# Three of seven block products with a 512-column operand of both residual parts, and two sums on VectorE in place of accumulation

## The chip, the cores and the metric

One core of a Trainium2 chip runs the whole program. The metric is the device time of one execution in microseconds; the median of three timed runs is taken. TensorE multiplies and adds up in PSUM (8 banks, each of 512 fp32 columns on 128 partitions), VectorE (DVE) and ScalarE (ACT) read PSUM and SBUF, GpSimd (POOL) SBUF only. The engines run their own queues in order and meet through semaphores.

## What is computed

The reference is a two-layer encoder over 512 tokens of width 1024. Each layer has two feed-forward halves (so four in all) around a mixer, and a gated embedding at its end. The change touches the feed-forward halves alone:

```python
def swiglu(h, w_gate, w_up, w_down):
    return (jax.nn.silu(h @ w_gate) * (h @ w_up)) @ w_down

h = h + 0.5 * swiglu(rms_norm(h, norms[i, 0]), ffn_w_gate[i, 0], ffn_w_up[i, 0], ffn_w_down[i, 0])
```

`w_gate` and `w_up` are 1024 x 2816, so gate and up together are 22 tiles of 128 rows each.

## The kernel before

**Precision.** Each fp32 operand is split into a high part (type fp32r, made by ACT with a copy) and a low part (the rest, made by DVE with a subtraction). A product of weight w and activation x is three matmuls: w_hi x_hi, w_hi x_lo, w_lo x_hi.

**Stages.** A feed-forward half f has an "up" stage of 22 tiles and a "down" stage. Six up tiles are plain (`in_chunk`, 512 columns). The other sixteen are *fast tiles*: gate and up weights of one tile form a 2 x 2 block matrix, which is multiplied with the 2 x 2 blocks of the normalised residual in seven block products in place of eight (Strassen's scheme). One block product is 4 blocks of 128 rows by 3 matmuls of 256 columns (`product`, L2284 to L2292). The sixteen tiles run as a static opening tile, one static tile, a hardware loop of two tiles per turn and, on DVE and ACT, a static end (`last_tile`).

**TensorE's order within a fast tile** (L2307 to L2328) is B11, T1, T2, B21, T3, B22, T4. B11, T2, T3, T4 add up in the tile's first bank; T1 and B22 in its right bank; B21 stands alone in its left bank. Two sets of three banks take turns. Since the first bank's partial sums are also needed, ACT copies them out between the products (`copy_part` 0, 1, 2, 3 after B11, T1, T2, T3), and TensorE waits for `copy_part` 0 before T2, for 2 before T3 and for 3 before T4.

**VectorE's order in a tile b** (`fast_tile`, L580) is: three weight sums for tile b+1 (`weight_sums`: w_sum 0:2 with 1024 elements, then two of 512 that each wait for the one before), low part of the sums T2 and T4 (`sums_lo` 0, which waits for ACT's high part), `gate_left`, low part of B11 and B21 (`own_lo` 0), `up_right`, low part of T1 and T3 (`sums_lo` 1), low part of B22 (`own_lo` 1), `up_left`, `product` (silu(gate) times up, written to `act_f`).

**ScalarE's order** (L1769) is: `copy_part` 0, 1, 2, high part of T2 and T4 (`sums_hi` 0, after the third weight sum and after T2), high part of B11 and B21 (`own_hi` 0), `copy_part` 3, `sums_hi` 1, `silu_left`, `own_hi` 1, `silu_right` (reads the first bank after T4). In `last_tile` (L1782) two copies of a finished tile's product, `act_high` 0 and 1, stand ahead of `copy_part` 0.

Each of these is one instruction on an in-order queue, so an instruction that waits holds all that stands behind it.

Of the kernel before, what the change touches and what calls it, by code (L numbers as in the profile page):

```python
# [24 lines left out]
P = 128  # L25
# [117 lines left out]
def encoder(nc, A, out):  # L143

    with ExitStack() as ctx:
        def sb(name, shape, dt=F32):
            where = nc.sbuf_base
            return ctx.enter_context(nc.sbuf_tensor(name, shape, dt)), where
# [3 lines left out]


        h, _ = sb("h", [P, KD, T])
        x_hi, at_x = sb("x_hi", [P, KD, T], F32R)
        x_lo, at_x_lo = sb("x_lo", [P, KD, T], F32R)
        act_hi, at_hi = sb("act_hi", [P, NF * T], F32R)
        act_lo, at_lo = sb("act_lo", [P, NF * T], F32R)
        raw, _ = sb("raw", [P, SLOTS, BLOCKS, P])
# [20 lines left out]
        def over(name, shape, where, dt=F32):  # L180

            return nc.alloc_sbuf_tensor_at(name, shape, dt, offset=where)
# [92 lines left out]
        act_f = over("act_f", [P, NF * T], at_lo)  # L275
        xn = over("xn", [P, KD, T], at_lo + 6 * tile_bytes)
        x_sum = over("x_sum", [P, 4, KH, HALF], at_lo + 14 * tile_bytes)
        xs_hi = over("xs_hi", [P, 4, KH, HALF], at_hi + 6 * tile_bytes, F32R)
        xs_lo = over("xs_lo", [P, 4, KH, HALF], at_hi + 14 * tile_bytes, F32R)
        corner_hi = over("corner_hi", [P, KH, HALF], at_hi + 2 * tile_bytes, F32R)  # L280
        corner_lo = over("corner_lo", [P, KH, HALF], at_hi + 4 * tile_bytes, F32R)
        part_sum = over("part_sum", [P, 4, T], at_x)
# [43 lines left out]
            "gate_scaled", "silu_done", "up_scaled", "prod_done", "act_hi_ready", "act_ready")}  # L326
        fast = {n: sem(f"fast_{n}") for n in (
            "x_gained", "x_normed", "x_sums", "x_hi", "x_ready", "w_sums", "t_hi",
            "t_ready", "product", "copied")}
        tab = sem("tab")  # L330
        tab_act = sem("tab_act")
        tab_pe = sem("tab_pe")
# [54 lines left out]
        def counted(each, f, i, b, n):  # L387

            return i * (2 * each) + (each * (b - PLAINS[f] + FAST_BEFORE[f]) + n)
# [11 lines left out]
        def banks_of(b):  # L401

            return ((5, 6, 7), (0, 1, 2))[b % 2]
# [41 lines left out]
        def act_low(dve, f, t):  # L445

            dve.wait_ge(ffn_sems["act_hi_ready"], t + 1 + NF * f)
            span = slice(t * T, (t + 1) * T)
            dve.tensor_tensor(act_lo[:, span], act_f[:, span], act_hi[:, span].bitcast(F32), SUB)\
               .then_inc(ffn_sems["act_ready"], 1)  # L450
# [5 lines left out]
        def ffn_up_dve(dve, f, n, first):  # L456
# [60 lines left out]
            def gate_left(i, b):  # L517
                dve.wait_ge(fast["product"], counted(5, f, i, b, 4))
                dve.wait_ge(fast["copied"], counted(4, f, i, b, 1))
                dve.tensor_tensor(t1[:, b % 2, 0:HALF], ps[:, banks_of(b)[1], 0:HALF],  # L520
                                  part_sum[:, 0, HALF:], ADD).then_inc(s["gate_scaled"], 1)

            def up_right(i, b):
                dve.wait_ge(fast["copied"], counted(4, f, i, b, 4))
# [2 lines left out]

            def up_left(i, b):
                dve.wait_ge(chunk_used, i * 4 + (first + 2 * b + 1))
                dve.tensor_tensor(t2[:, b % 2, 0:HALF], ps[:, banks_of(b)[2], 0:HALF],  # L530
                                  part_sum[:, 2, HALF:], ADD).then_inc(s["up_scaled"], 1)

            def product(i, b):
                dve.wait_ge(s["up_scaled"], i * 2 + (b + 1) + NF * f)
# [33 lines left out]
            def opening_tile():  # L568

                weight_sums(pair, 1)  # L570
                gate_left(pair, 0)
                own_lo(pair, 1, 0)
                sums_lo(pair, 1, 1)
                up_right(pair, 0)
                sums_lo(pair, 1, 0)
                own_lo(pair, 1, 1)
                up_left(pair, 0)
                product(pair, 0)

            def fast_tile(i, b):  # L580

                weight_sums(i, b + 1)
                sums_lo(i, b + 1, 0)
                gate_left(i, b)
                own_lo(i, b + 1, 0)
                up_right(i, b)
                sums_lo(i, b + 1, 1)
                own_lo(i, b + 1, 1)
                up_left(i, b)
                product(i, b)  # L590

            def last_tile(i, b):

                act_low(dve, f, 0)
                act_low(dve, f, 1)
                gate_left(i, b)
                split_lo(dve, first, FFN_UP)
                up_right(i, b)
                split_lo(dve, first, FFN_UP + 1)
                up_left(i, b)  # L600
                product(i, b)

            def passage_of_six():
# [1081 lines left out]
        def ffn_up_act(act, f, n, first, split=True):  # L1685
# [50 lines left out]
            def silu_right(i, b):  # L1736
                act.wait_ge(chunk_used, i * 4 + (first + 2 * b + 2))
                act.wait_ge(s["prod_done"], i * 2 + (b - 1) + NF * f)
                act.activation(t1[:, b % 2, HALF:], ps[:, banks_of(b)[0], 0:HALF], ACT.Silu)\
                   .then_inc(s["silu_done"], 1)  # L1740

            def residual_hi(o):
# [522 lines left out]
        def ffn_up_pe(pe, f, n, first):  # L2265
            s = ffn_sems

            if n == 4:
                for j in range(2):
                    in_chunk(pe, first, j, j, n=n, rows=range(KD - 1))  # L2270
                squares(pe, n)
                for j in range(2):
                    in_chunk(pe, first, j, j, n=n, rows=range(KD - 1, KD))
            plain = PLAINS[f]
            for j in range(2 if n == 4 else 0, 2 * plain):
                t, half = divmod(j, 2)
                before = [e for e in range(t) if PLAIN_BANKS[e] == PLAIN_BANKS[t]]
                if before:
                    pe.wait_ge(s[("gate_scaled", "up_scaled")[half]], before[-1] + 1 + NF * f)
                in_chunk(pe, first, j, PLAIN_BANKS[t][half], n=n if j == 0 else None)  # L2280
                if j == (0 if n in SQUARED else 1):
                    squares(pe, n)

            def product(bank, at, hi, lo, start, stop, done):  # L2284
                for k in range(KH):
                    cols = slice(k * P, (k + 1) * P)
                    for part, (w, x) in enumerate(((wf_hi, hi), (wf_hi, lo), (wf_lo, hi))):
                        last = pe.matmul(ps[:, bank, 0:HALF], w[:, at, cols], x[:, k],  # L2288
                                         start=(start and k == 0 and part == 0),
                                         stop=(stop and k == KH - 1 and part == 2),  # L2290
                                         skip_group_check=True)
                last.then_inc(done, 1)  # L2292

            def fast_tile(i, b):

                first_bank, left_bank, right_bank = banks_of(b)
                at = halves_of(first, b)

                def mixed(o):
                    return xs_hi[:, o], xs_lo[:, o]  # L2300

                def unmixed(o):
                    if o == 4:
                        return corner_hi, corner_lo
                    return quarter(x_hi, o), quarter(x_lo, o)

                pe.wait_ge(split_ready, i * 4 + (first + 2 * b + 1))  # L2307
                pe.wait_ge(fast["x_ready"], 7 * f + 5)
                pe.wait_ge(s["silu_done"], i * 2 + (b - 1) + NF * f)
                product(first_bank, at["B11"], *unmixed(4), True, False, fast["product"])  # L2310
                turned = isinstance(i, int) and 2 * i + b < plain + 2
                pe.wait_ge(fast["t_ready"], counted(2, f, i, b, 1 if turned else 2))
                pe.wait_ge(s["up_scaled"], i * 2 + (b - 1) + NF * f)
                product(right_bank, at["T1"], *mixed(0), True, False, fast["product"])
                if turned:
                    pe.wait_ge(fast["t_ready"], counted(2, f, i, b, 2))
                pe.wait_ge(fast["copied"], counted(4, f, i, b, 1))
                product(first_bank, at["T2"], *mixed(1), False, False, fast["product"])
                pe.wait_ge(fast["x_ready"], 7 * f + 6)
                pe.wait_ge(s["gate_scaled"], i * 2 + (b - 1) + NF * f)  # L2320
                product(left_bank, at["B21"], *unmixed(5), True, True, fast["product"])
                pe.wait_ge(fast["copied"], counted(4, f, i, b, 3))
                product(first_bank, at["T3"], *mixed(2), False, False, fast["product"])
                pe.wait_ge(split_ready, i * 4 + (first + 2 * b + 2))
                product(right_bank, at["B22"], *mixed(3), False, True, chunk_used)
                pe.wait_ge(fast["x_ready"], 7 * f + 7)
                pe.wait_ge(fast["copied"], counted(4, f, i, b, 4))
                product(first_bank, at["T4"], *unmixed(6), False, True, chunk_used)  # L2328

            fast_tile(plain // 2, 0)  # L2330
            fast_tile(plain // 2, 1)
            with pe.Fori(plain // 2 + 1, NF // 2, 1) as i:
                fast_tile(i, 0)
                fast_tile(i, 1)
# [601 lines left out]
```

## Time and profile before

| | |
|---|---|
| median of 3 runs (lowest to highest) | 1893.31 us (1892.08 to 1893.46) |
| profiled execution, its own time | 1893.9 us |
| its span, from the first to the last instruction | 1892.1 us |
| mean granted TensorE clock | 0.997 of 2.4 GHz |
| TensorE matmul busy | 1862.7 us (98%) |
| VectorE busy | 1342.0 us (71%) |
| ScalarE busy | 879.8 us (46%) |
| GpSimd busy | 261.3 us (14%) |
| share of the chain that ended last, by engine | PE 91%, DVE 6%, ACT 2%, POOL 1% |

Times are microseconds unless marked ns. PE is TensorE, PEld its weight loads, which overlap the matmuls. L12 is line 12 of the kernel before. The "chain" is followed back from the last instruction: at each step to what released it, or to the instruction before it on its engine. A matmul's duration in a row is its latency in the pipeline; how fast matmuls follow one another is read from the distance of their starts. The same holds for VectorE and ScalarE, where the next instruction can start a little before the one before has ended.

### The profile page before, as it was taken

The numbers are of one execution on the slowest core, as the hardware profiler recorded it, in microseconds if no ns is written. First come the engines' busy times: TensorE is split into PE (matmuls) and PEld (weight loads), VectorE is DVE, ScalarE is ACT, GpSimd is POOL, SyncE is SP. The second block draws the span as 40 slices with busy tenths as digits, with TensorE's granted clock in tenths as the row PEclk, the third lists the DMA queues.
The fourth block names the chain that finished last, engine by engine and source line by source line (L and its number), as shares of the span: only waits on it lengthen the run. The fifth ranks groups of instructions, "written<-read, shape, count | busy, mean of one in ns | idle before, by whom it ended". The sixth has DMA issues, their size and how long they took to land.

```text
span 1892.1 us, 30948 instructions
## 1 busy us (share of the span) xinstructions
PE 1862.7 (98%) x11274; PEld 1611.9 (85%) x11274; DVE 1342.0 (71%) x1957; ACT 879.8 (46%) x1475; POOL 261.3 (14%) x204
## 2 busy tenths in 40 slices
PE   8999999999999999999999999999989999999998
PEld 6899988777799998887899998877658899998886
DVE  8788788774878874357888864279984878874355
ACT  7455542245545554224455553234563645554222
POOL 0000001312100000224000001173243100000225
PEclk9999999999999999999999999999999999999999
DMA  5333333333223333323333343332101323333321
GB/s 179 90 111 96 105 104 104 95 99 91 78 87 104 111 102 120 105 74 100 101 91 99 111 122 95 94 109 68 56 1 45 94 88 108 111 102 121 102 76 56
DMA packets 56754, 179.90 MB, mean 95 GB/s; under 512 B 12144, under 2 KB 12144, under 8 KB 56656
## 3 DMA queue, kind: packets, MB, share of 16 engines
q1 hardware_dynamic: 54656, 173.69, 30.6%
q0 software_dynamic: 928, 3.02, 0.5%
q10 hardware_dynamic: 1088, 2.10, 0.3%
q8 instruction: 52, 0.85, 0.2%
q14 instruction: 30, 0.25, 0.0%
HBM read 175.04 MB, written 3.15 MB: 94 GB/s over the span
## 4 chain that ended last, share of the span: by engine, by line
PE 91%; DVE 6%; ACT 2%; POOL 1%; issue 0%; DMA 0%; DVEq 0%; SPq 0%; POOLq 0%; ACTq 0%
PE ps L2288 34%; PE ps L2250 26%; PE ps L2232 22%; PE ps L2736 2%; PE ps L2399 1%; PE ps L2635 1%; DVE sm L1265 1%; DVE work L1241 1%; POOL sumsq L1541 1%; PE ps L2685 1%; DVE stat L1239 1%; DVE x_lo L436 1%; PE ps L2654 0%; ACT prob L1970 0%; PE ps L2450 0%
## 5 line engine op out<-in xcount | busy, mean ns | idle before, releaser
L384 DVE TENSOR_TENSOR w_lo<-raw,w_hi 128x1024 fp32r<-128x1024 f32 x182 | 241.4, 1335 | 219.7 <-ACT w_hi L376 218.7
L376 ACT ACTIVATE w_hi<-raw 128x1024 fp32r<-128x1024 f32 x194 | 202.2, 1054 | 306.1 <-PE ps L2250 248.8
L2232 PE MATMUL ps<-x_hi,w_hi 128*128 128x512 f32 x704 | 282.7, 402 | 9.3 <-ACT w_hi L376 7.9
L2288 PE MATMUL ps<-xs_hi,w_hi 128*128 128x256 f32 x1024 | 290.1, 283 | 0.4
L2288 PE MATMUL ps<-xs_lo,w_hi 128*128 128x256 f32 x1024 | 289.8, 283 | 0.0
L2288 PE MATMUL ps<-xs_hi,w_lo 128*128 128x256 f32 x1024 | 289.7, 283 | 0.0
L2250 PE MATMUL ps<-act_hi,w_hi 128*128 (+1 forms) x720 | 280.4, 389 | 0.1
L2250 PE MATMUL ps<-act_lo,w_hi 128*128 (+1 forms) x720 | 280.2, 389 | 0.0
L2250 PE MATMUL ps<-act_hi,w_lo 128*128 (+1 forms) x720 | 280.1, 389 | 0.0
L2232 PE MATMUL ps<-x_hi,w_lo 128*128 128x512 f32 x704 | 275.3, 391 | 0.0
L2232 PE MATMUL ps<-x_lo,w_hi 128*128 128x512 f32 x704 | 275.1, 391 | 0.0
L506 DVE TENSOR_TENSOR w_lo<-w_sum,w_hi 128x1024 fp32r<-128x1024 f32 x128 | 156.4, 1222 | 90.8 <-ACT w_hi L1723 90.8
L2288 PEld LDWEIGHTS ps<-xs_hi,w_hi 128*128 128x128 f32 x1024 | 196.5, 192 | 1.1 <-issue 1.1
L2288 PEld LDWEIGHTS ps<-xs_lo,w_hi 128*128 128x128 f32 x1024 | 196.6, 192 | 0.0
L2288 PEld LDWEIGHTS ps<-xs_hi,w_lo 128*128 128x128 f32 x1024 | 196.6, 192 | 0.0
L1729 ACT ACTIVATE part_sum<-ps 128x256 f32<-128x256 f32 x256 | 98.3, 384 | 210.9 <-PE ps L2288 210.6
L2232 PEld LDWEIGHTS ps<-x_hi,w_hi 128*128 128x128 f32 x704 | 132.7, 189 | 42.9 <-ACT w_hi L376 7.9
L2250 PEld LDWEIGHTS ps<-act_hi,w_hi 128*128 128x128 f32 x720 | 135.2, 188 | 28.7 <-issue 0.9
L2250 PEld LDWEIGHTS ps<-act_hi,w_lo 128*128 128x128 f32 x720 | 135.2, 188 | 28.2
L2250 PEld LDWEIGHTS ps<-act_lo,w_hi 128*128 128x128 f32 x720 | 135.2, 188 | 27.8
L2232 PEld LDWEIGHTS ps<-x_hi,w_lo 128*128 128x128 f32 x704 | 132.7, 188 | 28.8 <-DVE w_lo L384 0.8
L2232 PEld LDWEIGHTS ps<-x_lo,w_hi 128*128 128x128 f32 x704 | 132.8, 189 | 28.5 <-issue 2.4
(406 smaller groups left out, 3510.3 us busy)
## 6 DMA issues: line engine op xcount, KB each, us to landing
raw<-in_weights SPq DMA_DIRECT2D x322, 512.0 KB, 3.7
h<-in_xT ACTq DMA_DIRECT2D x4, 512.0 KB, 6.6
out<-result SPq DMA_DIRECT2D x4, 512.0 KB, 3.0
p_raw<-in_pT POOLq DMA_DIRECT2D x2, 512.0 KB, 4.0
scratch_u<-u_sc SPq DMA_DIRECT2D x1, 512.0 KB, 6.7
u_grp<-scratch_u SPq DMA_DIRECT2D x1, 512.0 KB, 4.2
scratch_y<-y_grp SPq DMA_DIRECT2D x2, 256.0 KB, 3.0
y_ch<-scratch_y SPq DMA_DIRECT2D x1, 512.0 KB, 3.5
```

Of the source, the lines that this page charges most:

```text
L376: act.activation(w_hi[:, slot], raw[:, slot], ACT.Copy).then_inc(hi_ready, 1)
L384: dve.tensor_tensor(w_lo[:, slot], raw[:, slot], w_hi[:, slot].bitcast(F32), SUB)\
L436: dve.scalar_tensor_tensor(out=x_lo[:, k], in0=h[:, k], scalar=gains[:, n, k:k + 1], in1=x_hi[:, k].bitcast(F32), op0=MULT, op1=SUB)\
L506: dve.tensor_tensor(wf_lo[:, at], src, wf_hi[:, at].bitcast(F32), SUB)\
L1239: do(dve.max(out=top, in_=src))
L1241: do(dve.match_replace(out=rest, in_to_replace=top, in_values=src, imm_value=LOWEST))
L1265: dve.tensor_tensor_reduce(out=sm[s % len(sm)][:, 0:keys], in0=ps[:, 2 + s % 2, 0:keys], in1=added, scale=-SCALE, scalar=-LOWEST, op0=ADD, ...
L1729: act.activation(part_sum[:, which, HALF:], ps[:, bank, 0:HALF], ACT.Copy).then_inc(fast["copied"], 1)
L2232: last = pe.matmul(ps[:, bank], w[:, slot, k], x[:, k], start=(k == 0 and part == 0), stop=(k == KD - 1 and part == 2))
L2250: last = pe.matmul(ps[:, (4, 0)[group] + d], w[:, slot, b], x(row), start=(start and row == 0 and part == 0), stop=(stop_ and row == 1 and ...
L2288: last = pe.matmul(ps[:, bank, 0:HALF], w[:, at, cols], x[:, k], start=(start and k == 0 and part == 0), stop=(stop and k == KH - 1 and pa ...
L2736: last = pe.matmul(ps[:, bank], w[:, slot, b], x[:, rows], start=(m == 0 and row == 0 and part == 0), stop=(m == 1 and row == 1 and part = ...
```

## The change

The high and low parts of the residual lie side by side in one tensor. Products B21, B22 and T4 take both as one 512-column operand for the w_hi matmul, so that w_hi x_hi goes to the left half of the bank and w_hi x_lo to the right half; w_lo x_hi (256 columns) is added to the left half. The two halves are then added: on VectorE with a second sum in `gate_left` (after B21) and in `up_left` (after B22), each of which waits for the first; after T4 ACT copies the bank's right half to SBUF, VectorE adds the left half (`gate_right`), and ACT applies silu to that. `product` moves from the end of a tile to behind the three weight sums of the next. The opening tile ends in `gate_right` in place of `product`, the last has both.

```diff
-        x_hi, at_x = sb("x_hi", [P, KD, T], F32R)
-        x_lo, at_x_lo = sb("x_lo", [P, KD, T], F32R)
+        x_parts, at_x = sb("x_parts", [P, 2, KD, T], F32R)
+        x_hi, x_lo = x_parts[:, 0], x_parts[:, 1]
...
             def gate_left(i, b):
                 dve.wait_ge(fast["product"], counted(5, f, i, b, 4))
                 dve.wait_ge(fast["copied"], counted(4, f, i, b, 1))
-                dve.tensor_tensor(t1[:, b % 2, 0:HALF], ps[:, banks_of(b)[1], 0:HALF],
-                                  part_sum[:, 0, HALF:], ADD).then_inc(s["gate_scaled"], 1)
+                left = ps[:, banks_of(b)[1]]
+                dve.tensor_tensor(t1[:, b % 2, 0:HALF], left[:, 0:HALF],
+                                  part_sum[:, 0, HALF:], ADD).then_inc(fast["folded"], 1)
+                dve.wait_ge(fast["folded"], counted(2, f, i, b, 1))
+                dve.tensor_tensor(t1[:, b % 2, 0:HALF], left[:, HALF:], t1[:, b % 2, 0:HALF],
+                                  ADD).then_inc(s["gate_scaled"], 1)
+
+            def gate_right(i, b):
+                dve.wait_ge(fast["half_copied"], counted(1, f, i, b, 1))
+                dve.tensor_tensor(t1[:, b % 2, HALF:], ps[:, banks_of(b)[0], 0:HALF],
+                                  t1[:, b % 2, HALF:], ADD).then_inc(fast["right_scaled"], 1)
...
             def up_left(i, b):
                 dve.wait_ge(chunk_used, i * 4 + (first + 2 * b + 1))
-                dve.tensor_tensor(t2[:, b % 2, 0:HALF], ps[:, banks_of(b)[2], 0:HALF],
-                                  part_sum[:, 2, HALF:], ADD).then_inc(s["up_scaled"], 1)
+                right = ps[:, banks_of(b)[2]]
+                dve.tensor_tensor(t2[:, b % 2, 0:HALF], right[:, 0:HALF],
+                                  part_sum[:, 2, HALF:], ADD).then_inc(fast["folded"], 1)
+                dve.wait_ge(fast["folded"], counted(2, f, i, b, 2))
+                dve.tensor_tensor(t2[:, b % 2, 0:HALF], right[:, HALF:], t2[:, b % 2, 0:HALF],
+                                  ADD).then_inc(s["up_scaled"], 1)
...
             def fast_tile(i, b):
 
+                dve.wait_ge(fast["t_ready"], counted(2, f, i, b, 2))
                 weight_sums(i, b + 1)
+                product(i, b - 1)
                 sums_lo(i, b + 1, 0)
                 gate_left(i, b)
                 own_lo(i, b + 1, 0)
@@ -587,10 +603,11 @@
                 sums_lo(i, b + 1, 1)
                 own_lo(i, b + 1, 1)
                 up_left(i, b)
-                product(i, b)
+                gate_right(i, b)
...
             def silu_right(i, b):
                 act.wait_ge(chunk_used, i * 4 + (first + 2 * b + 2))
                 act.wait_ge(s["prod_done"], i * 2 + (b - 1) + NF * f)
-                act.activation(t1[:, b % 2, HALF:], ps[:, banks_of(b)[0], 0:HALF], ACT.Silu)\
+                act.activation(t1[:, b % 2, HALF:], ps[:, banks_of(b)[0], HALF:], ACT.Copy)\
+                   .then_inc(fast["half_copied"], 1)
+                act.wait_ge(fast["right_scaled"], counted(1, f, i, b, 1))
+                act.activation(t1[:, b % 2, HALF:], t1[:, b % 2, HALF:], ACT.Silu)\
                    .then_inc(s["silu_done"], 1)
...
+            def paired(bank, at, both, start, stop, done):
+                for k in range(KH):
+                    cols = slice(k * P, (k + 1) * P)
+                    pe.matmul(ps[:, bank], wf_hi[:, at, cols], both[:, :, k],
+                              start=(start and k == 0), stop=False, skip_group_check=True)
+                    last = pe.matmul(ps[:, bank, 0:HALF], wf_lo[:, at, cols], both[:, 0, k],
+                                     start=False, stop=(stop and k == KH - 1),
+                                     skip_group_check=True)
+                last.then_inc(done, 1)
...
-                product(left_bank, at["B21"], *unmixed(5), True, True, fast["product"])
+                paired(left_bank, at["B21"], both(5), True, True, fast["product"])
...
-                product(right_bank, at["B22"], *mixed(3), False, True, chunk_used)
+                paired(right_bank, at["B22"], xs_parts[:, :, 3], False, True, chunk_used)
...
-                product(first_bank, at["T4"], *unmixed(6), False, True, chunk_used)
+                paired(first_bank, at["T4"], both(6), False, True, chunk_used)
```

## Rows read from the trace of the kernel before

**Rows 1.** The page's chain that ended last, by line, shares of the span.

```profile
PE ps L2288 34%; PE ps L2250 26%; PE ps L2232 22%; PE ps L2736 2%; PE ps L2399 1%; PE ps L2635 1%; DVE sm L1265 1%; DVE work L1241 1%; POOL sumsq L1541 1%; PE ps L2685 1%; DVE stat L1239 1%; DVE x_lo L436 1%; PE ps L2654 0%; ACT prob L1970 0%; PE ps L2450 0%
```

**Rows 2.** The chain in order of time: start us, us, what, times.

```profile
77.26 2.87 PE ps L2288 x24
80.13 0.11 issue
80.23 158.62 PE ps L2288 x1320
...
238.86 43.55 PE ps L2250 x192
```

**Rows 3.** Stretch of the first fast tiles: length, busy time of each engine, PEclk, DMA.

```profile
77.00:239.00 162.00, 161.89 (x1348) 161.64 (x1347) 133.67 (x177) 92.73 (x163) 0.00 (x0) 1.00 0.34 102
```

**Rows 4.** Timeline, PE: start us, us, engine, line, operation, out<-in. B21's first matmul.

```profile
192.61 0.28 PE L2288 MATMUL ps<-x_hi,w_hi 128*128 128x256 f32 x1
```

**Rows 5.** Timeline of ACT in the same tile.

```profile
192.81 0.38 ACT L1729 ACTIVATE part_sum<-ps 128x256 f32<-128x256 f32 x1 [1.05 <-PE ps L2288]
193.09 1.05 ACT L1723 ACTIVATE w_hi<-w_sum 128x1024 fp32r<-128x1024 f32 x1
...
196.92 0.41 ACT L1734 ACTIVATE t<-t 128x256 f32<-128x256 f32 x1
197.23 0.62 ACT L1713 ACTIVATE w_hi<-raw 128x512 fp32r<-128x512 f32 x1
```

**Rows 6.** Timeline of DVE in the same tile, inside the loop.

```profile
194.18 1.23 DVE L506 TENSOR_TENSOR w_lo<-w_sum,w_hi 128x1024 fp32r<-128x1024 f32 x1 [1.55 <-ACT w_hi L1723]
195.32 0.42 DVE L520 TENSOR_TENSOR t<-ps,part_sum 128x256 f32<-128x256 f32 x1
195.65 1.22 DVE L514 TENSOR_TENSOR w_lo<-raw,w_hi 128x1024 fp32r<-128x1024 f32 x1
196.78 0.42 DVE L525 TENSOR_TENSOR t<-part_sum 128x256 f32<-128x256 f32 x1
197.12 1.22 DVE L506 TENSOR_TENSOR w_lo<-w_sum,w_hi 128x1024 fp32r<-128x1024 f32 x1
198.26 0.69 DVE L514 TENSOR_TENSOR w_lo<-raw,w_hi 128x512 fp32r<-128x512 f32 x1
198.86 0.42 DVE L530 TENSOR_TENSOR t<-ps,part_sum 128x256 f32<-128x256 f32 x1
199.42 0.69 DVE L536 SCALAR_TENSOR_TENSOR act_f<-t 128x512 f32 x1
200.03 1.22 DVE L491 TENSOR_TENSOR w_sum<-raw 128x1024 f32<-128x1024 f32 x1
201.28 0.69 DVE L495 TENSOR_TENSOR w_sum<-w_sum,raw 128x512 f32<-128x512 f32 x1
202.01 0.69 DVE L498 TENSOR_TENSOR w_sum<-w_sum,raw 128x512 f32<-128x512 f32 x1
```

**Rows 7.** Timeline of DVE in the opening tile, ahead of the loop.

```profile
86.18 1.23 DVE L506 TENSOR_TENSOR w_lo<-w_sum,w_hi 128x1024 fp32r<-128x1024 f32 x1 [0.17 <-ACT w_hi L1723]
...
89.39 0.42 DVE L530 TENSOR_TENSOR t<-ps,part_sum 128x256 f32<-128x256 f32 x1
89.84 0.69 DVE L536 SCALAR_TENSOR_TENSOR act_f<-t 128x512 f32<-128x512 f32 x1
```

**Rows 8.** Timeline where T2 of the opening tile waits for ACT's copy.

```profile
79.73 0.82 ACT L1729 ACTIVATE part_sum<-ps 128x256 f32<-128x256 f32 x2
...
79.85 0.28 PE L2288 MATMUL ps<-xs_hi,w_lo 128*128 128x256 f32 x1
...
80.23 0.35 PE L2288 MATMUL ps<-xs_hi,w_hi 128*128 128x256 f32 x1
80.43 0.28 PE L2288 MATMUL ps<-xs_lo,w_hi 128*128 128x256 f32 x1
```

**Rows 9.** Timeline of ACT ahead of the last fast tile's first copy.

```profile
229.09 1.15 ACT L1677 ACTIVATE act_hi<-act_f 128x512 fp32r<-128x512 f32 x2
```

More of the change, by code:

```diff
@@ L154, in encoder @@
         h, _ = sb("h", [P, KD, T])
-        x_hi, at_x = sb("x_hi", [P, KD, T], F32R)
-        x_lo, at_x_lo = sb("x_lo", [P, KD, T], F32R)
+        x_parts, at_x = sb("x_parts", [P, 2, KD, T], F32R)
+        x_hi, x_lo = x_parts[:, 0], x_parts[:, 1]
+        at_x_lo = at_x + 4 * KD * T
         act_hi, at_hi = sb("act_hi", [P, NF * T], F32R)
@@ L277, in encoder @@
         x_sum = over("x_sum", [P, 4, KH, HALF], at_lo + 14 * tile_bytes)
-        xs_hi = over("xs_hi", [P, 4, KH, HALF], at_hi + 6 * tile_bytes, F32R)
-        xs_lo = over("xs_lo", [P, 4, KH, HALF], at_hi + 14 * tile_bytes, F32R)
+        xs_parts = over("xs_parts", [P, 2, 4, KH, HALF], at_hi + 6 * tile_bytes, F32R)
+        xs_hi, xs_lo = xs_parts[:, 0], xs_parts[:, 1]
         corner_hi = over("corner_hi", [P, KH, HALF], at_hi + 2 * tile_bytes, F32R)
@@ L328, in encoder @@
             "x_gained", "x_normed", "x_sums", "x_hi", "x_ready", "w_sums", "t_hi",
-            "t_ready", "product", "copied")}
+            "t_ready", "product", "copied", "folded", "half_copied", "right_scaled")}
         tab = sem("tab")
@@ L577, in opening_tile @@
                 up_left(pair, 0)
-                product(pair, 0)
+                gate_right(pair, 0)
             def fast_tile(i, b):
+                dve.wait_ge(fast["t_ready"], counted(2, f, i, b, 2))
                 weight_sums(i, b + 1)
+                product(i, b - 1)
                 sums_lo(i, b + 1, 0)
@@ L589, in fast_tile @@
                 up_left(i, b)
-                product(i, b)
+                gate_right(i, b)
             def last_tile(i, b):
+                product(i, b - 1)
                 act_low(dve, f, 0)
@@ L600, in last_tile @@
                 up_left(i, b)
+                gate_right(i, b)
                 product(i, b)
@@ L2300, in mixed, with corner, both @@
                     return xs_hi[:, o], xs_lo[:, o]
[L2302 to L2305, printed above, removed]
+                def corner():
+                    return corner_hi, corner_lo
+                def both(o):
+                    return x_parts[:, :, KH:KD, slice(HALF, T) if o == 6 else slice(0, HALF)]
                 pe.wait_ge(split_ready, i * 4 + (first + 2 * b + 1))
@@ L2309, in fast_tile @@
                 pe.wait_ge(s["silu_done"], i * 2 + (b - 1) + NF * f)
-                product(first_bank, at["B11"], *unmixed(4), True, False, fast["product"])
+                product(first_bank, at["B11"], *corner(), True, False, fast["product"])
                 turned = isinstance(i, int) and 2 * i + b < plain + 2
```

## Prediction

> **What bounds the kernel now.** I read the chain by line first: nearly all of it is matmul, and the block products of the fast tiles (L2288) are its largest share, 34% [rows 1]. Then the chain in order of time: a fast stage is 24 matmuls, one break of 0.1 us and 1320 matmuls that follow each other without another break, 161.6 us in all [rows 2]; four stages look like this. 16 tiles of 84 matmuls make 1344 of them, 0.120 us each, so a tile takes TensorE 10.08 us. The 512-column matmuls of the down stage take 43.55 / 192 = 0.2268 us, those within a steady stretch 0.2267 [rows 2]. So two of 256 columns cost 0.240 where one of 512 costs 0.2267: every pair that is merged saves 0.0133 us. Third, the stage by engine: DVE is busy 133.7 of 162 us, ACT 92.7, the granted clock is 1.00 (the 2.4 GHz level), POOL is idle and DMA has a share of 0.34 [rows 3]. DVE has room, but not much, and the question is whether its room lies where the change wants it. For that I read one tile on each engine [rows 4 to 6]. DVE waits once in it, 1.55 us ahead of `sums_lo` 0, and that wait is for ACT's high part, which itself waited for `copy_part` 2, that is for T2's end on TensorE [rows 5, 6].
>
> **What it removes.** Three products of a tile lose 4 matmuls of 256 columns each as separate instructions: 12 x 0.0133 = 0.16 us a tile, so TensorE alone would need 9.92 us. Over 64 tiles that is 10.2 us. B21, B22 and T4 take 1.387 us each in place of 1.44. `product` leaves the end of DVE's tile (its next starts 0.61 after it, and it starts 0.56 after `up_left`) and moves into the gap behind the third weight sum. That costs nothing: the third sum's end to `sums_lo` 0 is at least 0.04 + 1.09 us (ACT's high part in between, 193.09 to 194.18), and the product needs 0.69 [rows 5, 6]. It waits for silu of the tile before, which is over by then (below).
>
> **What it adds.** The new instructions are of the 256-column kind with a PSUM input. DVE's take 0.42 us, and an instruction that needs no wait starts 0.33 after them (195.32 to 195.65); one that waits for their result starts 0.45 after (`up_left` to `product` in the opening, 89.39 to 89.84) [rows 6, 7]. So `gate_left` takes 0.45 + 0.33 in place of 0.33, `up_left` likewise, and `gate_right` 0.33. ACT gets a PSUM copy of 0.38 and a silu of 0.41 from SBUF [rows 5] where it had one silu. The new waits matter more than the work. ACT now waits between copy and silu for `gate_right`, and behind that silu stands `copy_part` 0 of the next tile, for which TensorE waits ahead of T2. So a loop closes that was open: T2, copy 2, high sums on ACT, all of DVE's tile, `gate_right`, silu, copy 0, T2 of the next tile.
>
> **The length of that loop**, from T2's end (B21's first matmul, 192.61 [rows 4]) as zero: copy 2 starts at 0.20, high sums at 0.48, `sums_lo` 0 at 1.57, `gate_left` 2.71, its second sum 3.16, `own_lo` 0 at 3.49, `up_right` 4.62, `sums_lo` 1 at 4.96, `own_lo` 1 at 6.10, `up_left` 6.70, its second sum 7.15, `gate_right` 7.48, its end 7.90 [rows 5 to 7]. None of these DVE steps waits for TensorE: T4 ends at 1.387 + 1.44 + 1.387 + 1.387 = 5.60, and its copy is over at 6.2. Then silu starts at 7.94 (0.04, as from ACT's 194.14 to DVE's 194.18), copy 0 at 8.25 (0.31 after a silu of this size, 196.92 to 197.23) and ends at 8.63 [rows 5, 6]. For the last link there is one case in the trace: in the opening tile copy 0 ends at 80.11, T2's first matmul starts at 80.23, and its second 0.20 later, not 0.12 [rows 8]. So T2 starts 0.12 after the copy and loses another 0.08: 8.83. TensorE by itself would start the next T2 at 9.92 - 1.44 = 8.48. It stands still for 0.35 us, and a tile takes 8.83 + 1.44 = 10.27 us, 0.19 more than now. Each pause is of a fraction of a microsecond, and the clock stays at 1.00 in a stretch that has such a break in it [rows 3, 8]; I give it no price. DVE and ACT alone form a second loop (third weight sum, high sums, DVE's tile, weight sums of the next): 5.91 from `sums_lo` 0 to `gate_right`, 0.33 + 1.25 + 0.73 to the third sum, 0.69 + 0.04 + 1.09 to the next `sums_lo` 0, in all 10.04 [rows 5, 6]. It is also longer than 9.92, but the first loop hides it.
>
> **The ends of a stage.** Opening: `up_left` at 89.39 becomes 89.67 (0.45 more, less the 0.17 that DVE waited there) [rows 7]; second sum 90.12, `gate_right` 90.45 to 90.87, silu 90.91, copy 0 at 91.22 to 91.60, T2 of the second tile at 91.80. TensorE would be there at 80.31 + 7.04 (rest of the first tile) + 2.88 = 90.23: a pause of 1.57. Last tile: two `act_high`, 1.15 - 0.62 = 0.52 us apart, stand between silu and copy 0 [rows 9]; today slack hides them, now they add 1.04 to the pause of 0.35. Behind the stage nothing new is late: the low parts of activation tiles 2 and 3 are ready some 0.9 us later than now, about 4.9 us into the down stage, and its second chunk begins at 24 x 0.2267 = 5.44.
>
> **Sum.** A stage: -16 x 0.16 + 1.57 + 13 x 0.35 + 1.39 = -2.56 + 7.51 = +4.95 us. Four stages: +19.8. The profiled execution (span 1892.1, its own time 1893.9) would become 1913.7; the median of the runs lies 0.6 lower, so 1913.1.
>
> **Bounds of the unknown costs.** The restart loss may be 0 instead of 0.08, and a wait for one's own result 0.42 (nothing beyond the duration) instead of 0.45: the pause is 0.21, a stage +2.9, the total 1905. A gain below that would need less than the duration, which is the second rival. Upwards, each of the two waits may take 0.1 more (between 0.45 and the 0.56 of the loop [rows 6]): pause 0.55, a stage +8, the total 1925. How fast 512 columns in two pieces of 256 stream is in no row. Between 0.2133 (512 columns at 2.4 GHz) and 0.240 it changes little: TensorE outside T2 is not in the loop, so slower pairs only shorten the pause. At 0.240 the pause is 0.19 and a stage +5.1. I take 0.2267.
>
> **Rivals.** (1) *Copy 0 is not late.* If ACT and DVE went through their tile in under 8.48 us, TensorE would never wait and the whole 10.2 us would be saved: 1883.1, faster. It decides at 0.35 us of 8.83. For it speaks only that DVE is idle for 18% of the stage [rows 3]; against it, that the steps add up without one gap in them [rows 5 to 7]. 6%. (2) *A second sum starts as early as an independent instruction*, 0.33 after the first. The loop is 0.24 shorter, the pause 0.11, a stage -2.56 + 1.33 + 13 x 0.11 + 1.15 = +1.35: 1898.7; with no restart loss +0.2 a stage, 1894. Three waits of this kind speak against it [rows 6, 7]: 0.45, 1.25 (after an instruction whose independent successor starts at 1.14) and 0.73 (0.60). The Trainium skill (VectorE: DVE Perf Modes, The DRAIN you can't avoid) says otherwise: in a chain of copies a semaphore after each "costs nothing extra here". By that page the sum would be this rival's 1898.7; in this trace the wait costs 0.11 to 0.13, and the measurement decides. 10%, half of it within 0.2%. (3) *Waits inside the hardware loop are dearer.* In the loop `product` starts 0.56 after `up_left` [rows 6], in the opening 0.45 [rows 7]. If that is the wait and not the product's moving address, both second sums pay it: pause 0.57, a stage +8.3, 1926. Against it, weight sum 2 waits for its own result in the loop and starts 0.03 after its end [rows 6]. 8%. (4) *The pairing does not save anything on TensorE*: by the line above, 1914, which the total could not tell from the forecast; it is part of its chance.
>
> **How the numbers follow.** The loop as worked out, with its bounds: 76%, 1905 to 1925. A measurement of this kernel can tell 0.2% (3.8 us) from no change, so same is 1889.5 to 1897.1. Faster 0.06 (rival 1), same 0.06 (half of rival 2 and a little), slower 0.88. The range 1902 to 1924 leaves out rivals 1, 2 and 3, and takes in nearly all of the main case.
>
> **What would show it.** In the profile after: a short break in the chain ahead of each T2, with ACT's copy 0 ending just before it; tiles 10.27 us apart; DVE's wait ahead of `sums_lo` 0 shorter, `product` in it; ACT's silu released by `gate_right` on DVE; stages of about 166.5 us; the 512-column matmuls of L2288's successor at 0.227. The prediction is wrong if tiles are 9.92 apart (rival 1), if the second sums start 0.33 after the first (rival 2) or 0.56 (rival 3), or if the stage grows elsewhere, such as by late weights from DMA.

## Result

The changed kernel takes 1914.67 us (median of 4 runs, 1912.41 to 1915.22) against 1893.37: ratio 1.0111, 95% interval 1.0099 to 1.0123. It is 21 us slower; 1913.1 was forecast. Its profiled execution has a span of 1912.2 us, 20.1 more than before, at the same clock of 0.997.

The page's chain, by engine and by line (shares of the span), after the change; it answers to [rows 1]:

```profile
PE 75%; DVE 15%; ACT 4%; issue 4%; POOL 1%; DMA 0%; DVEq 0%; ACTq 0%; SPq 0%; POOLq 0%
PE ps L2271 25%; PE ps L2253 22%; PE ps L2309 13%; PE ps L2318 5%; PE ps L2320 3%; DVE w_lo L515 2%; PE ps L2768 2%; DVE w_lo L507 2%; ACT w_hi L1741 1%; PE ps L2431 1%; PE ps L2667 1%; DVE sm L1283 1%; DVE t L522 1%; DVE t L530 1%; ACT part_sum L1747 1%
```

Before, matmul made up 91% of the chain and the block products 34%. Now L2309 (single products), L2318 and L2320 (the 512- and 256-column matmuls of a pair) have 21% together, and DVE and ACT have the rest of the fast stages: their low parts, their sums, the high sums and `part_sum`. The chain no longer stays on TensorE; it goes round.

The chain in order of time, one piece out of each turn of the hardware loop (two tiles): start, length, what. It answers to the unbroken 158.62 us of [rows 2]:

```profile
143.11 1.70 PE ps L2309 x12
...
163.65 1.70 PE ps L2309 x12
...
184.18 1.69 PE ps L2309 x12
...
204.71 1.70 PE ps L2309 x12
```

Each is a T2, and they lie 20.53 us apart: 10.27 a tile (10.22 and 10.32 by turns).

**Where the time came from.** From the first matmul of the first fast tile to the first of the down stage it took 161.60 us in each of the four stages before. After, it is 166.36 in the first (77.26 to 243.62), 166.70, 166.33 and 166.34 in the others, 19.3 us more in all. The rest of the kernel takes 1246.5 us where it took 1245.7. So the loss lies in the fast stages. The waits of that execution (engine, line and tile that waited, for whom: us in total, times, longest) name the two ends of it:

```profile
PE ps L2309 <- ACT part_sum L1747: 9.0, 9, 1.2
```

```profile
ACT t L1760 <- DVE t L530: 104.6, 64, 2.7
```

TensorE waits for the copy of a partial sum, and ACT, once a tile, for `gate_right` (L530) ahead of silu (L1760). The list of TensorE's waits shows only nine, eight of them at the two ends of the four stages; the short ones are seen in the timeline. This is one tile on ACT (start, us, engine, line, operation, out<-in, idle before and releaser):

```profile
193.65 0.42 ACT L1760 ACTIVATE t<-t 128x256 f32<-128x256 f32 x1 [1.59 <-DVE t L530]
193.97 0.88 ACT L1747 ACTIVATE part_sum<-ps 128x256 f32<-128x256 f32 x2
196.13 0.39 ACT L1747 ACTIVATE part_sum<-ps 128x256 f32<-128x256 f32 x1 [1.28 <-PE ps L2309]
196.41 1.05 ACT L1741 ACTIVATE w_hi<-w_sum 128x1024 fp32r<-128x1024 f32 x1
...
203.87 0.42 ACT L1760 ACTIVATE t<-t 128x256 f32<-128x256 f32 x1 [1.67 <-DVE t L530]
204.27 0.80 ACT L1747 ACTIVATE part_sum<-ps 128x256 f32<-128x256 f32 x2
```

The same tile on DVE:

```profile
196.12 0.68 DVE L550 SCALAR_TENSOR_TENSOR act_f<-t 128x512 f32 x1
197.49 1.23 DVE L507 TENSOR_TENSOR w_lo<-w_sum,w_hi 128x1024 fp32r<-128x1024 f32 x1 [0.69 <-ACT w_hi L1741]
198.64 0.42 DVE L522 TENSOR_TENSOR t<-ps,part_sum 128x256 f32<-128x256 f32 x1
199.09 0.42 DVE L525 TENSOR_TENSOR t<-ps,t 128x256 f32<-128x256 f32 x1
199.43 1.21 DVE L515 TENSOR_TENSOR w_lo<-raw,w_hi 128x1024 fp32r<-128x1024 f32 x1
200.56 0.42 DVE L535 TENSOR_TENSOR t<-part_sum 128x256 f32<-128x256 f32 x1
200.90 1.22 DVE L507 TENSOR_TENSOR w_lo<-w_sum,w_hi 128x1024 fp32r<-128x1024 f32 x1
202.03 0.68 DVE L515 TENSOR_TENSOR w_lo<-raw,w_hi 128x512 fp32r<-128x512 f32 x1
202.63 0.41 DVE L541 TENSOR_TENSOR t<-ps,part_sum 128x256 f32<-128x256 f32 x1
203.08 0.42 DVE L544 TENSOR_TENSOR t<-ps,t 128x256 f32<-128x256 f32 x1
203.43 0.41 DVE L530 TENSOR_TENSOR t<-ps,t 128x256 f32<-128x256 f32 x1
203.76 1.21 DVE L492 TENSOR_TENSOR w_sum<-raw 128x1024 f32<-128x1024 f32 x1
```

And on TensorE: T1's last matmul and the first three of T2, B21's first matmul, and of B22 the first pair, the start of the second and the end (T4's first matmul):

```profile
194.15 0.28 PE L2309 MATMUL ps<-xs_parts,w_lo 128*128 128x256 f32 x1
194.39 0.51 PE L2309 MATMUL ps<-xs_parts,w_hi 128*128 128x256 f32 x2
194.73 0.28 PE L2309 MATMUL ps<-xs_parts,w_lo 128*128 128x256 f32 x1
...
195.93 0.40 PE L2318 MATMUL ps<-x_parts,w_hi 128*128 128x512 f32 x1
...
198.78 0.40 PE L2318 MATMUL ps<-xs_parts,w_hi 128*128 128x512 f32 x1
199.02 0.28 PE L2320 MATMUL ps<-xs_parts,w_lo 128*128 128x256 f32 x1
199.14 0.39 PE L2318 MATMUL ps<-xs_parts,w_hi 128*128 128x512 f32 x1
...
200.20 0.40 PE L2318 MATMUL ps<-x_parts,w_hi 128*128 128x512 f32 x1
```

Matmuls of 256 columns follow one another every 0.12 us, and T2 starts 0.24 after T1's last: a pause of 0.12 us here, and of 0.22 in the other tile of a turn.

Read it round the loop, from T2's end at 195.93: copy 2 at 196.13, high sums at 196.41, `sums_lo` 0 at 197.49, then DVE without a gap to `gate_right` at 203.43, silu at 203.87, copy 0 at 204.27, the next T2 at 204.71. `product` (L550) sits in the wait ahead of `sums_lo` 0, which has shrunk from 1.55 us [rows 6] to 0.69. B22 takes 200.20 - 198.78 = 1.42 us where 12 matmuls took 1.44.

### The profile page after: what moved, and what is told of

Same layout as the page of the kernel before. It is cut to its first block, busy times and chain, and to the rows that moved or that the text cites. A ratio compares the mean times of both kernels' runs of the same rounds, so it can differ in the third digit from the quotient of the medians.

```text
span 1912.2 us, 29812 instructions
## 1 busy us (share of the span) xinstructions
PE 1873.3 (98%) x10506; PEld 1575.6 (82%) x10506; DVE 1412.7 (74%) x2149; ACT 900.9 (47%) x1539; POOL 261.1 (14%) x204
## 4 chain that ended last, share of the span: by engine, by line
PE 75%; DVE 15%; ACT 4%; issue 4%; POOL 1%; DMA 0%; DVEq 0%; ACTq 0%; SPq 0%; POOLq 0%
PE ps L2271 25%; PE ps L2253 22%; PE ps L2309 13%; PE ps L2318 5%; PE ps L2320 3%; DVE w_lo L515 2%; PE ps L2768 2%; DVE w_lo L507 2%; ACT w_hi L1741 1%; PE ps L2431 1%; PE ps L2667 1%; DVE sm L1283 1%; DVE t L522 1%; DVE t L530 1%; ACT part_sum L1747 1%
## 5 line engine op out<-in xcount | busy, mean ns | idle before, releaser
L2253 PE MATMUL ps<-x_parts,w_hi 128*128 128x512 f32 x1408 | 444.1, 397 | 8.8 <-ACT w_hi L377 7.4
L2253 PEld LDWEIGHTS ps<-x_parts,w_hi 128*128 128x128 f32 x1408 | 262.9, 189 | 71.0 <-ACT w_hi L377 7.4
L2309 PE MATMUL ps<-xs_parts,w_hi 128*128 128x256 f32 x1536 | 290.7, 287 | 10.9 <-ACT part_sum L1747 9.0
L2253 PE MATMUL ps<-x_parts,w_lo 128*128 128x512 f32 x704 | 275.6, 391 | 0.0
L2309 PEld LDWEIGHTS ps<-xs_parts,w_hi 128*128 128x128 f32 x1536 | 237.5, 190 | 25.2 <-ACT part_sum L1747 15.8
L2309 PE MATMUL ps<-xs_parts,w_lo 128*128 128x256 f32 x768 | 217.2, 283 | 0.0
L2318 PE MATMUL ps<-x_parts,w_hi 128*128 128x512 f32 x512 | 186.5, 398 | 0.0
L2253 PEld LDWEIGHTS ps<-x_parts,w_lo 128*128 128x128 f32 x704 | 132.8, 189 | 28.9 <-DVE w_lo L385 0.8
L2309 PEld LDWEIGHTS ps<-xs_parts,w_lo 128*128 128x128 f32 x768 | 146.2, 190 | 0.0
L2320 PE MATMUL ps<-x_parts,w_lo 128*128 128x256 f32 x512 | 143.6, 280 | 0.0
L1741 ACT ACTIVATE w_hi<-w_sum 128x1024 fp32r<-128x1024 f32 x128 | 134.6, 1052 | 7.2 <-PE ps L2253 7.2
```

What stands on the lines that cost most here:

```text
L1741: act.activation(wf_hi[:, at], src, ACT.Copy).then_inc(fast["t_hi"], 1)
L2253: last = pe.matmul(ps[:, bank], w[:, slot, k], x[:, k], start=(k == 0 and part == 0), stop=(k == KD - 1 and part == 2))
L2318: pe.matmul(ps[:, bank], wf_hi[:, at, cols], both[:, :, k], start=(start and k == 0), stop=False, skip_group_check=True)
L2320: last = pe.matmul(ps[:, bank, 0:HALF], wf_lo[:, at, cols], both[:, 0, k], start=False, stop=(stop and k == KH - 1), skip_group_check=True)
```

## Experiments

Every experiment is told with the length of its first fast stage, measured in its trace as above (161.60 before, 166.36 after), since the rest of the kernel hardly moves. Ratios are to the kernel before, with 95% intervals.

### Each half of the change alone

Pairs only: VectorE and ScalarE as before, so w_hi x_lo of three products is left out.

```diff
-                left = ps[:, banks_of(b)[1]]
-                dve.tensor_tensor(t1[:, b % 2, 0:HALF], left[:, 0:HALF],
-                                  part_sum[:, 0, HALF:], ADD).then_inc(fast["folded"], 1)
-                dve.wait_ge(fast["folded"], counted(2, f, i, b, 1))
-                dve.tensor_tensor(t1[:, b % 2, 0:HALF], left[:, HALF:], t1[:, b % 2, 0:HALF],
-                                  ADD).then_inc(s["gate_scaled"], 1)
+                dve.tensor_tensor(t1[:, b % 2, 0:HALF], ps[:, banks_of(b)[1], 0:HALF],
+                                  part_sum[:, 0, HALF:], ADD).then_inc(s["gate_scaled"], 1)
...
-                gate_right(i, b)
+                product(i, b)
```

> TensorE of the changed kernel (B21, B22 and T4 paired) with VectorE and ScalarE as before: the sums of the two halves are left out, so w_hi x_lo of these three products is missing from the output. Nothing closes the loop, so TensorE should run a fast tile without a pause. In the trace of the changed kernel a paired product takes 1.41 to 1.42 us where the prediction had 1.387 and a product of 12 takes 1.44. Theory A (a pair of 512 and 256 columns takes 0.353): a tile 10.00, the total 64 x 0.08 = 5 us under the kernel before, 1888. Theory B (the prediction's 0.2267 for 512 columns holds when nothing waits): a tile 9.92, 10 us less, 1883. If the pauses of the changed kernel came from the pairing itself, this one would be slower than before.

Measured: 1888.10 us (8 runs), ratio 0.9972 (0.9962 to 0.9983). The stage is 160.32 us, so each of 48 paired products saves 1.28 / 48 = 0.027 us. Theory A holds; the pairing by itself is a gain, half as large as the prediction's rate would have it.

Sums only: the other half, with all products in 256 columns.

```diff
-                paired(left_bank, at["B21"], both(5), True, True, fast["product"])
+                product(left_bank, at["B21"], x_hi[:, KH:KD, 0:HALF], x_lo[:, KH:KD, 0:HALF],
+                        True, True, fast["product"])
...
-                dve.tensor_tensor(t1[:, b % 2, 0:HALF], left[:, HALF:], t1[:, b % 2, 0:HALF],
+                dve.tensor_tensor(t1[:, b % 2, 0:HALF], left[:, 0:HALF], t1[:, b % 2, 0:HALF],
```

> VectorE and ScalarE as in the changed kernel, TensorE with all seven products in 12 matmuls of 256 columns; the added sums read the left half a second time in place of the right, so these sums are wrong by a factor. Theory A (the loop T2, copy 2, high sums, VectorE's tile, gate_right, silu, copy 0, T2 sets the pace, and of TensorE only T2 is in it): a tile stays at 10.27, the pause ahead of T2 shrinks by what the pairs no longer save, the total is 1914 to 1916. Theory B (TensorE's own time adds to the pace): 5 us more than the changed kernel, 1920. If pairing were the cause of the loss, this would be near 1893.

Measured: 1915.18 us (4 runs), ratio 1.0115 (1.0100 to 1.0131), stage 166.46. With and without pairs the kernel takes the same time. That is the sign of a loop that TensorE's other products are not part of: what they save is returned as a longer pause ahead of T2. The traces show it: the pause is 0.05 and 0.15 us by turns here, 0.12 and 0.22 in the changed kernel.

### The same instruction inside and outside the loop

```diff
+            def extra():
+                dve.tensor_tensor(rstd[:, 0:HALF], rstd[:, HALF:], rstd[:, HALF:], ADD)
...
                 own_lo(i, b + 1, 1)
+                extra()
                 up_left(i, b)
```

> The changed kernel with one more 256-element sum on VectorE in each of 14 tiles a stage, just ahead of up_left; nobody uses its result. Theory A (the loop): the instruction is in the loop and costs its 0.33 us in each of 14 x 4 tiles, 18.5 us, total 1933. Theory B (VectorE has room, it waits 0.7 us in each tile ahead of sums_lo 0, and the loss is elsewhere): no change, 1915.

Measured: 1933.83 us (4 runs), ratio 1.0211 (1.0195 to 1.0227). The stage is 171.10, 4.74 more than without, or 0.34 for each of 14 tiles.

```diff
                 product(i, b - 1)
+                extra()
                 sums_lo(i, b + 1, 0)
```

> The same extra sum, as often, but behind product and ahead of sums_lo 0, where VectorE waits 0.7 us for ScalarE. Theory A (the loop): this place is parallel to ScalarE's high sums, so it is hidden, total 1915. Theory B (VectorE's total work sets the pace): the same 18.5 us as in the other place, 1933.

Measured: 1914.89 us (4 runs), ratio 1.0116 (1.0101 to 1.0132), stage 166.41: free. The two traces show the same work in two places. Inside the loop (timeline of DVE):

```profile
195.03 0.68 DVE L515 TENSOR_TENSOR w_lo<-raw,w_hi 128x512 fp32r<-128x512 f32 x1
195.64 0.42 DVE L583 TENSOR_TENSOR rstd<-rstd 128x256 f32<-128x256 f32 x1
195.97 0.42 DVE L541 TENSOR_TENSOR t<-ps,part_sum 128x256 f32<-128x256 f32 x1
```

In the gap:

```profile
195.58 0.68 DVE L550 SCALAR_TENSOR_TENSOR act_f<-t 128x512 f32 x1
196.18 0.42 DVE L583 TENSOR_TENSOR rstd<-rstd 128x256 f32<-128x256 f32 x1
196.94 1.23 DVE L507 TENSOR_TENSOR w_lo<-w_sum,w_hi 128x1024 fp32r<-128x1024 f32 x1 [0.34 <-ACT w_hi L1745]
```

In the gap the idle time falls from 0.69 to 0.34 and nothing else moves; ahead of `up_left` everything behind it comes 0.33 later. So it is not DVE's total work that sets the pace but its place.

### Opening the loop

T4 undone alone, so that silu waits for no other engine than TensorE:

```diff
-                paired(first_bank, at["T4"], both(6), False, True, chunk_used)
+                product(first_bank, at["T4"], x_hi[:, KH:KD, HALF:T], x_lo[:, KH:KD, HALF:T],
+                        False, True, chunk_used)
...
-                act.activation(t1[:, b % 2, HALF:], ps[:, banks_of(b)[0], HALF:], ACT.Copy)\
-                   .then_inc(fast["half_copied"], 1)
-                act.wait_ge(fast["right_scaled"], counted(1, f, i, b, 1))
-                act.activation(t1[:, b % 2, HALF:], t1[:, b % 2, HALF:], ACT.Silu)\
+                act.activation(t1[:, b % 2, HALF:], ps[:, banks_of(b)[0], 0:HALF], ACT.Silu)\
```

> The changed kernel with one part undone: T4 is again 12 matmuls of 256 columns, and silu reads PSUM, with no copy and no gate_right. B21 and B22 stay paired, with their second sums, and product stays behind the weight sums. Theory A (the wait of ACT for gate_right closes the loop): no pause ahead of T2. VectorE and ScalarE alone need 10.04 - 0.33 = 9.71, TensorE 10.08 - 2 x 0.027 = 10.03 a tile: total 1893.4 - 3.4 = 1890. Theory B (the second sums are what costs): still over 1900.

Measured: 1890.40 us (11 runs), ratio 0.9986 (0.9977 to 0.9995), stage 160.89. With both second sums still on DVE there is no loss, so they alone were not its cause; the silu that waits for `gate_right` was needed for it. They do make up 0.9 us of the loop's length, and by the sum of the prediction a loop shorter by that would leave no pause; no run has the closed loop without them.

All three pairs kept, and only an order turned round on ScalarE:

```diff
             def fast_tile(i, b):
                 copy_part(i, b, 0)
+                silu_whole(i, b - 1)
                 copy_part(i, b, 1)
...
             def silu_right(i, b):
...
                    .then_inc(fast["half_copied"], 1)
+
+            def silu_whole(i, b):
                 act.wait_ge(fast["right_scaled"], counted(1, f, i, b, 1))
```

> The changed kernel with one order turned round on ScalarE: copy 0 of the next tile stands ahead of the silu that waits for gate_right (in the last tile also ahead of the two act_high). The computation is the same. Theory A (copy 0 behind that silu closes the loop): the pause ahead of T2 is gone, also the 1.5 us of the opening tile and the 1.4 of the last one. What is left is the loop of VectorE and ScalarE alone, 10.04 a tile by the prediction's steps, against 10.00 for TensorE: the total is 64 x 0.04 = 2.6 us under the kernel before, some 1891. Theory B (the silu itself or the extra copy holds something else): the total stays near 1915.

Measured: 1897.49 us (10 runs), ratio 1.0023 (1.0014 to 1.0033), stages of 161.66, 162.37, 161.76 and 162.34. This gives back 17 of the 21 us with the same work, so theory A holds for the pauses; but the total is 6.5 us over what was expected. DVE's tile is as I had it: `sums_lo` 0 starts at 184.47, 194.53 and 204.59, 10.06 apart (10.04 expected). What I left out is the opening. TensorE's waits in that trace:

```profile
PE ps L2314 <- DVE w_lo L515: 1.1, 4, 0.3
```

One wait in each stage, for the low part of B11 and B21: DVE comes late out of the opening. The kernel before has the same late start but a DVE round of 9.53 us (`sums_lo` 0 at 94.31 and 103.84) against TensorE's 10.08, and catches up; at 10.06 against 10.00 it never does. So a stage is TensorE's 160.3, about 0.5 for the opening and 14 x 0.06. This reading was not tested alone, but the next run fits it: it makes DVE's round shorter than TensorE's tile. The second and the fourth stage take 0.6 us more than the other two. There, in each of the five turns of the hardware loop, DVE's first weight sum starts 0.45 to 0.47 us after `gate_right` (609.22 to 609.68), and in the first and the third stage always 0.33 to 0.34; 5 x 0.12 is the 0.6. What that sum waits for had come more than 1.7 us earlier. Why the turn takes longer in these two stages stays open.

The two second sums moved one place on, beside that order:

```diff
                 gate_left(i, b)
                 own_lo(i, b + 1, 0)
+                gate_left_low(i, b)
...
                 up_left(i, b)
                 gate_right(i, b)
+                up_left_low(i, b)
```

> As the run before, and the second sum of gate_left stands behind own_lo 0, that of up_left behind gate_right, so that neither follows directly on the instruction whose result it needs. Each should save the 0.12 us by which such a wait is longer than the plain distance of 0.33. Theory A: VectorE and ScalarE alone would need 10.04 - 0.24 = 9.80 a tile, TensorE 10.00 is the bound, total 1893.4 - 5.1 = 1888. Theory B (the second sums were not in the way): as the run before, 1891.

Measured: 1889.56 us (11 runs), ratio 0.9983 (0.9974 to 0.9992), stage 160.48, within 0.16 of pairs only. Theory A. In its trace no sum follows on the one it needs, and each 256-element instruction takes 0.33 to 0.34 until the next:

```profile
197.94 0.42 DVE L544 TENSOR_TENSOR t<-ps,part_sum 128x256 f32<-128x256 f32 x1
198.27 0.42 DVE L533 TENSOR_TENSOR t<-ps,t 128x256 f32<-128x256 f32 x1
198.60 0.42 DVE L550 TENSOR_TENSOR t<-ps,t 128x256 f32<-128x256 f32 x1
198.93 1.23 DVE L492 TENSOR_TENSOR w_sum<-raw 128x1024 f32<-128x1024 f32 x1
```

In the changed kernel the same three took 0.45, 0.35 and 0.33 (202.63 to 203.76).

### Why a pair saves half of what it should

```diff
                     pe.matmul(ps[:, bank], wf_hi[:, at, cols], both[:, :, k],
                               start=(start and k == 0), stop=False, skip_group_check=True)
+                for k in range(KH):
+                    cols = slice(k * P, (k + 1) * P)
                     last = pe.matmul(ps[:, bank, 0:HALF], wf_lo[:, at, cols], both[:, 0, k],
```

> As the run before, and within a paired product the four matmuls of 512 columns come first, then the four of 256. Theory A (512 and 256 columns in turns cost more than in steady runs): 0.2267 and 0.120 each, a tile 9.92, total 1893.4 - 10.2 = 1883. Theory B (the operand in two pieces of 256 columns costs 0.2347 wherever it stands): no change from the run before, 1888.

Measured: 1887.77 us (8 runs), ratio 0.9974 (0.9964 to 0.9985), stage 159.93. Neither theory: 0.55 us a stage better than in turns, where 1.28 was expected of A and nothing of B. It is the fastest kernel here that leaves out nothing, 5.3 us under the kernel before. To part the two causes, three variants of the kernel with pairs only. Grouped order, as in the diff above:

> The kernel with pairs only, with the four matmuls of 512 columns of a paired product ahead of its four of 256. The sums of the halves are left out. It measures the pair's price by the length of a fast stage: 161.60 us without pairs, 160.32 with pairs in turns, which is 1.28 / 48 = 0.027 less for each of 48 paired products where steady rates would give 0.053. Theory A (the turns between 512 and 256 columns cost): six of eight turns are gone, the stage is 159.3. Theory B (the operand in two pieces costs): 160.32 again. The run with the second sums spread and grouped order lay between, at 159.93.

An unbroken operand, first in turns, then also grouped:

```diff
-                    pe.matmul(ps[:, bank], wf_hi[:, at, cols], both[:, :, k],
+                    whole = xs_parts[:, 0].rearrange("p o k c -> p (o k c)")[:, k * T:(k + 1) * T]
+                    pe.matmul(ps[:, bank], wf_hi[:, at, cols], whole,
```

> The kernel with pairs only, in turns, where the 512-column operand is one unbroken run of 512 columns of another tensor instead of two pieces of 256 (so these products are wrong, and the sums of the halves are left out). Theory B (the two pieces cost): the stage is 161.60 - 48 x 0.053 = 159.0. Theory A: 160.32 as with two pieces.

> Both at once: unbroken operand, and the four of 512 columns ahead of the four of 256 (these products are wrong, the sums of the halves are left out). If turns and pieces each cost a part, this one reaches the steady rates, a stage of 159.0 to 159.1; if the first 512-column matmul behind one of 256 always costs more, it stays above that.

| pairs only, first fast stage | two pieces | one unbroken run |
|---|---|---|
| 512 and 256 in turns | 160.32 | 160.32 |
| four of 512, then four of 256 | 159.68 | 159.68 |

(Totals of the last three: grouped 1885.57, unbroken in turns 1888.40, unbroken and grouped 1884.88 us; ratios 0.9964, 0.9977 and 0.9963, all intervals below 1.) The two pieces of the operand cost nothing: theory B is out. The order does cost, as theory A has it, but grouping gives back 0.64 us of a stage and not the 1.0 that was expected: a paired product saves 1.28 / 48 = 0.027 us in turns and 1.92 / 48 = 0.040 grouped, where the steady rates give 0.053. Both at once stay above the steady rates, too. The grouped trace shows where the rest is (timeline of TensorE, pairs grouped):

```profile
191.62 1.09 PE L2303 MATMUL ps<-x_parts,w_hi 128*128 128x512 f32 x4
192.55 0.63 PE L2307 MATMUL ps<-x_parts,w_lo 128*128 128x256 f32 x4
193.02 0.40 PE L2294 MATMUL ps<-xs_parts,w_hi 128*128 128x256 f32 x2
```

Four of 512 take 0.93 us, 0.2325 each, and four of 256 take 0.47, 0.1175 each; 0.2267 and 0.120 are the rates of long runs. The 512s lose 0.023 us by that and the 256s gain 0.010, which is the 0.013 between 0.053 and 0.040. So in groups as short as four, matmuls are not paced as in a long run. What in TensorE does this stays open.

## Why the prediction was right, point by point

- **The loop and its length.** Forecast from T2's end: high sums 0.48, `sums_lo` 0 at 1.57, `gate_left` 2.71, `own_lo` 0 at 3.49, `up_left` 6.70, `gate_right` 7.48, silu 7.94. In the trace: 0.48, 1.56, 2.71, 3.50, 6.70, 7.50, 7.94. The tile came out at 10.27 as forecast, though TensorE by itself needed 10.00 where 9.92 was forecast. That this loop is the cause is shown by the pair of runs with one instruction in two places, and by the two that open it.
- **Its last link was right in sum only, by luck.** Forecast: copy 0 0.31 after silu, T2 0.12 after its end, and 0.08 lost on the restart. In the trace silu to copy 0 is 0.32 in one tile and 0.40 in the other of each turn of the hardware loop (193.65 to 193.97, 203.87 to 204.27), T2 starts 0.04 to 0.06 after the copy, and its first two matmuls take 0.34, not 0.24 (194.39 to 194.73). The differences, -0.07, +0.02, +0.01 and every second tile +0.08, cancel. The 0.40 stands where the hardware loop turns on ACT, five times a stage; in the second stage it is 0.47 to 0.50, which is about the 0.35 us by which this stage is the longest.
- **A wait for one's own result costs 0.45, in the loop too** (198.64 to 199.09, 202.63 to 203.08). That refutes rivals 2 and 3: the distance of 0.56 before `product` was not the price of such a wait; what in `product` makes it, no run shows. The Trainium skill (VectorE: DVE Perf Modes, The DRAIN you can't avoid) found, on a chain of eight copies, that a semaphore after each "costs nothing extra here". That does not carry over to this case: 0.45 against 0.33.
- **The ends of a stage.** Forecast T2 of the second tile 14.7 us after the stage begins (91.80 - 77.09); it starts 14.6 after (91.83 - 77.26). A stage is 4.76 longer in the trace, 4.95 in the sum. Term by term, measured and forecast: TensorE's saving -1.28 and -2.56, the opening 1.43 and 1.57, thirteen tiles 3.35 and 4.55, the last tile 1.26 and 1.39.
- **The term that was mis-sized** is the saving of a pair: 0.16 us a tile by the steady rates, 0.08 in fact (stage 160.32). It did not show in the total, as rival 4 said, since TensorE outside T2 only shortens or lengthens the pause: the saving of a stage was put 1.28 us too high and its pauses 1.47 too high. Had rival 1 come true, the gain would have been 5 us, not 10.
- **`product` at no cost** held: it lies in the gap, which at 0.69 us had room for still another instruction.

## What to carry to other kernels

Before an engine is given more work, look for who waits behind the new wait, not for how idle the engine is: here DVE had 18% to spare, and 1.2 us of sums and one wait on ACT's queue turned a chain with slack into a closed loop that cost 1.1%. Follow such a loop once round with distances of starts from the rows; if it is longer than the bound engine's own tile, nothing saved on that engine counts. The cure can be an order: the same work with one copy ahead of the silu and the sums apart from what they need runs 0.2% faster than the kernel before (ratio 0.9983), and 0.3% with the matmuls of a pair grouped as well (0.9974).

## What the runs showed of the hardware

- Matmuls of 512 and 256 columns in turns take 0.353 us a pair where long runs of each would give 0.347; grouped in fours it is 0.350. Whether the 512 columns are one run or two pieces makes no difference to 0.01 us in a stage of 160.
- A VectorE instruction of 256 elements that waits for the result of the one before starts 0.45 us after it, with one operand in PSUM; one that does not wait starts 0.33 after it, with operands in PSUM or SBUF. With all operands in SBUF it is 0.73 against 0.60 for 512 elements and 1.25 against 1.14 for 1024 [rows 6].
- After a pause, TensorE's first two matmuls of 256 columns take 0.34 us where they take 0.24 in a run. Pauses of 0.12 to 0.22 us once in 10 us left the granted clock at the 2.4 GHz level (1.00 in the stage, 0.997 over the span).
- Two instructions between which the hardware loop turns can start further apart than elsewhere, with no wait between them: on ScalarE 0.40 us (0.47 to 0.50 in one stage) where it is 0.32 in the tiles without a turn, on VectorE 0.45 to 0.47 in two of four stages where it is 0.33 in the others.
